# A hybrid DeltaNet and MoBA block: gates and branches computed feature-major, in tiles of 128 features

## The reference, cut to what matters

```python
h = rms_norm(x, norm_pre_w)
proj = jnp.einsum('bsd,df->bsf', h, w_in)          # heads, z paths, 2 x 1024 gate logits
...
gates = sigmoid(gate_logits + b_gate).reshape(bsz, s, 2, d)
pa = jnp.einsum('bsf,fd->bsd', ya, w_branch[0])
pb = jnp.einsum('bsf,fd->bsd', yb, w_branch[1])
merged = gates[:, :, 0] * pa + gates[:, :, 1] * pb
out = jnp.einsum('bsd,de->bse', merged, w_out)
return x + rms_norm(out, norm_post_w)
```

## Time and profile before

| | us |
|---|---|
| median of 3 runs (lowest, highest) | 358.39 (357.66, 358.43) |
| profiled execution, whole | 358.36 |
| profiled execution, span of its instructions | 356.6 |
| PE, DVE, ACT busy | 347.2, 269.1, 219.5 |

### The profile page before, as it was taken

One profiled execution on the slowest core, in us unless ns is written; L12 is line 12 of the kernel. 1 busy time (PEld: TensorE's weight loads), 2 busy tenths in 40 slices (PEclk: granted clock), 3 DMA queues, 4 the chain that ended last, 5 costly groups with the idle time before them and its releaser, 6 DMA issues.

```text
span 356.6 us, 6674 instructions
## 1 busy us (share of the span) xinstructions
PE 347.2 (97%) x2387; PEld 317.9 (89%) x2387; DVE 269.1 (75%) x550; ACT 219.5 (62%) x484; POOL 58.6 (16%) x114
## 2 busy tenths in 40 slices
PE   6999999999999999999999999999999999999993
PEld 5889997888899999999999999999998888888882
DVE  2969877599997868978788797878977657566744
ACT  5778795443447767686867867777776544425421
POOL 1533534500050000300203021030300101000011
PEclk9999999999999999999999999999999999999998
DMA  8766956893599476445744566465534735766333
GB/s 266 175 193 174 342 168 213 232 344 124 141 271 236 122 191 161 123 119 151 203 120 124 135 181 156 119 156 148 169 120 137 247 118 171 245 234 235 123 114 118
DMA packets 76206, 63.48 MB, mean 178 GB/s; under 512 B 4724, under 2 KB 62478, under 8 KB 76174
## 3 DMA queue, kind: packets, MB, share of 16 engines
q1 hardware_dynamic: 73838, 59.37, 57.0%
q0 software_dynamic: 1152, 3.30, 3.2%
q10 hardware_dynamic: 1184, 0.39, 0.5%
HBM read 61.46 MB, written 1.59 MB: 177 GB/s over the span
## 4 chain that ended last, share of the span: by engine, by line
PE 74%; DVE 10%; DMA 6%; ACT 4%; issue 3%; SPq 1%; POOL 1%; DVEq 0%; POOLq 0%; ACTq 0%
PE banks L1387 35%; PE banks L1442 18%; PE banks L1649 6%; DVE w_lo L919 4%; DMA raw<-in_w_in_dram 3%; DMA th_E<-g_rows 2%; PE banks L1405 2%; DVE acc L992 2%; ACT w_hi L670 1%; DVE sub L1056 1%; ACT th_E L711 1%; DMA g_rows<-grow 1%; PE banks L1537 1%; PE banks L1554 1%; PE banks L1543 1%
## 5 line engine op out<-in xcount | busy, mean ns | idle before, releaser
L919 DVE TENSOR_TENSOR w_lo<-raw,w_hi 128x1024 fp32r<-128x1024 f32 x102 | 124.1, 1224 | 47.6 <-ACT w_hi L670 46.9
L670 ACT CAST w_hi<-raw 128x1024 fp32r<-128x1024 f32 x103 | 107.3, 1048 | 30.6 <-PE banks L1442 13.9
L1387 PE MATMUL banks<-h_hi,w_hi 128*128 128x256 f32 x440 | 64.0, 288 | 0.1
L1387 PE MATMUL banks<-h_lo,w_hi 128*128 128x256 f32 x440 | 59.4, 277 | 0.0
L1387 PE MATMUL banks<-h_hi,w_lo 128*128 128x256 f32 x440 | 59.2, 277 | 0.0
L1387 PEld LDWEIGHTS banks<-h_hi,w_hi 128*128 128x128 f32 x440 | 55.2, 189 | 0.7 <-DVE acc L992 0.3
L1387 PEld LDWEIGHTS banks<-h_lo,w_hi 128*128 128x128 f32 x440 | 54.1, 188 | 0.0
L1387 PEld LDWEIGHTS banks<-h_hi,w_lo 128*128 128x128 f32 x440 | 54.1, 188 | 0.0
L992 DVE SCALAR_TENSOR_TENSOR acc<-banks,vec,acc 128x255 f32<-128x255 f32 (+2 forms) x72 | 34.5, 479 | 3.0 <-ACT acc L789 1.3
L616 POOL TENSOR_TENSOR so<-so,rnq 128x2 f32<-128x2 f32 x8 | 2.0, 253 | 162.8 <-ACT junk L856 162.8
L789 ACT ACTIVATE acc<-banks,vec 128x256 f32<-128x256 f32 x16 | 7.6, 475 | 16.9 <-PE banks L1387 16.9
(11 more groups left out here) (257 smaller groups left out, 606.5 us busy)
## 6 DMA issues: line engine op xcount, KB each, us to landing
raw<-in_w_in_dram SPq DMA_DIRECT2D x80, 512.0 KB, 5.1
raw<-in_w_branch_dram SPq DMA_DIRECT2D x16, 512.0 KB, 4.7
raw<-in_w_out_dram SPq DMA_DIRECT2D x8, 512.0 KB, 4.2
xin<-in_x_dram SPq DMA_DIRECT2D x2, 512.0 KB, 3.9
th_E<-g_rows POOLq DMA_DIRECT2D x2, 512.0 KB, 7.3
bias<-bias_rows POOLq DMA_DIRECT2D x1, 1024.0 KB, 7.4
raw<-in_x_dram SPq DMA_DIRECT2D x2, 512.0 KB, 3.7
out_dram<-xin SPq DMA_DIRECT2D x4, 256.0 KB, 2.0
```

What stands on the lines that cost most here:

```text
L670: nc.scalar.copy(w_hi[:, t % SLOTS, :], raw[:, t % SLOTS, :]).then_inc(s_hi, 1)
L919: v.tensor_tensor(w_lo[:, t % SLOTS, cols], raw[:, t % SLOTS, cols], w_hi[:, t % SLOTS, cols].bitcast(F32), ALU.subtract).then_inc(s_lo, 1)
L1387: last = mm(ps, w, r, start=part == 0 and k == 0, stop=part == 2 and k == KT - 1)
```

## The change

Gate and branch tiles become feature-major: each is 128 features, loaded as columns of 512 bytes a row, formed by `third` in banks 0 and 1 in turn, as the heads' tiles are. The gate's bias is then a column: b_gate is loaded as 16 more rows at the start, turned with the other small vectors, scaled by 0.5 on the vector engine, and given to ScalarE's tanh as its bias; the tanh reads the bank directly, 128x256 at a time, 16 times. `gate_front` and its row loads go. Both branches are multiplied tile by tile, the sum is feature-major as it stands, `turn_m` goes, and `m_part` and `m_rest` split 128x256 of it a tile. Waits change with the banks.

```diff
-GATE_ROWS = [(60, 61), (72, 73), (88, 91), (3 * BRANCH0, 3 * BRANCH0 + 1)]
-GATE_TANH = [62, 74, 94, 3 * BRANCH0 + 3]
-M_TURN = 3 * BRANCH0 + 40
...
-        gate_banks = [(bank[0], bank[1]), (bE, bF), (bA, bD), (bC, bank[0])]
-        branch_banks = [(bank[1], bA), (bB, bD), (bE, bF), (bank[0], bank[1])]
-        m_banks = [(bA, bB), (bank[0], bank[1])]
...
+        bgate = sb("bgate", [P, 2 * KT])
...
+        def gate(g):
+            return th_a[:, g, :] if g < KT else th_E[:, g - KT, :]
...
@@ SyncE
             sp.dma_start(rows[R_PRE:R_ON, :], norm_pre_w.rearrange("(t p) -> t p", p=P)).then_inc(s_rows, 16)
-            sp.dma_start(rows[R_ON:ROWS, :], dn_onorm_w.rearrange("(t p) -> t p", p=P)).then_inc(s_rows, 16)
+            sp.dma_start(rows[R_GATE:ROWS, :], b_gate.rearrange("(t p) -> t p", p=P)).then_inc(s_rows, 16)
+            sp.dma_start(rows[R_ON:R_GATE, :], dn_onorm_w.rearrange("(t p) -> t p", p=P)).then_inc(s_rows, 16)
...
-                if n == 12:
-                    sp.wait_ge(s_bd_p, 1)
-                    for group in range(3):
-                        part = b_gate[512 * group:512 * group + 512].rearrange("(a n) -> a n", a=1)
-                        sp.dma_start(early_rows[group], part.to_broadcast([P, 512])).then_inc(s_rows_e, 16)
             for g in range(EARLY):
-                gate_load(GATES_A + g, g // 4, g % 4)
+                load(GATES_A + g, GATES_A + g, w_tile(COL_GATE + P * g))
...
-                half, branch, q = t // 4 % 2, 1 - t // 8, t % 4
-                group_load(BRANCH0 + t, w_branch[branch][256 * q:256 * q + 256, 512 * half:512 * half + 512])
+                k = t % KT
+                load(BRANCH0 + t, BRANCH0 + t, w_branch[1 - t // KT][:, P * k:P * k + P].rearrange("(k p) n -> p k n", p=P))
...
@@ GpSimd
-                if g == HEADS - 1:
-                    pool.wait_ge(s_sc, 2 * HEADS)
-                    pool.dma_start(late_rows, b_gate[1536:2048].rearrange("(a n) -> a n", a=1).to_broadcast([P, 512])
-                                   ).then_inc(s_rows_l, 16)
...
@@ ScalarE
-            def gate_tanh(group):
-                sa.wait_ge(s_gate_b, 2 * group + 2)
-                ac(th[group], th[group], ACT.Tanh, scale=0.5).then_inc(s_gate_th, 1)
-            def m_parts(half, b):
-                sa.wait_ge(s_m_turned, half + 1)
-                k = 4 * half + 2 * b
-                nc.scalar.copy(m_hi[:, k:k + 2, :], m_banks[half][b].rearrange("p (k n) -> p k n", k=2)).then_inc(s_m_hi, 1)
+            def gate_tanh(g):
+                n = GATES_A + g if g < EARLY else GATES_B + g - EARLY
+                sa.wait_ge(s_tile, n + 1)
+                if g == 0:
+                    sa.wait_ge(s_vec, 3)
+                ac(gate(g), bank[n % 2][:, 0:SEQ], ACT.Tanh, bias=bgate[:, g:g + 1], scale=0.5).then_inc(s_gate_th, 1)
+            def m_part(k):
+                sa.wait_ge(s_m_sum, k + 1)
+                nc.scalar.copy(m_hi[:, k:k + 1, :], one(gate(KT + k))).then_inc(s_m_hi, 1)
...
-                for group in range(4):
-                    if S == GATE_TANH[group]:
-                        gate_tanh(group)
-                if S in (M_TURN + 1, M_TURN + 2):
-                    m_parts(0, S - M_TURN - 1)
+                for g in range(2 * KT):
+                    if S == 3 * (GATES_A + g if g < EARLY else GATES_B + g - EARLY) + 3:
+                        gate_tanh(g)
+                for k in range(KT - 1):
+                    if S == 3 * (BRANCH0 + KT + k) + 4:
+                        m_part(k)
                 if part == 1:
                     split_hi(n + LEAD, n + LEAD, (n + LEAD) // SLOTS + 1)
+            m_part(KT - 1)
             for k in range(KT - LEAD):
                 split_hi(OUT0 + k + LEAD, k + LEAD, (OUT0 + k + LEAD) // SLOTS + 1)
...
@@ the vector engine
+            v.tensor_scalar(bgate[:], vec[:, R_GATE:ROWS], 0.5, None, ALU.mult).then_inc(s_vec, 1)
...
+            def second_branch(k):
+                n = BRANCH0 + k
+                ve.wait_ge(s_gate_th, KT + k + 1)
+                ve.wait_ge(s_tile, n + 1)
+                v.scalar_tensor_tensor(out=gate(KT + k), in0=gate(KT + k), scalar=1.0, in1=bank[n % 2][:, 0:SEQ],
+                                       op0=ALU.add, op1=ALU.mult).then_inc(s_m_b, 1)
+            def first_branch(k):
+                n = BRANCH0 + KT + k
+                ve.wait_ge(s_tile, n + 1)
+                v.scalar_tensor_tensor(out=gate(k), in0=gate(k), scalar=1.0, in1=bank[n % 2][:, 0:SEQ],
+                                       op0=ALU.add, op1=ALU.mult).then_inc(s_m_a, 1)
+                ve.wait_ge(s_m_b, k + 1)
+                ve.wait_ge(s_m_a, k + 1)
+                v.tensor_tensor(gate(KT + k), gate(KT + k), gate(k), ALU.add).then_inc(s_m_sum, 1)
+            def m_rest(k):
+                ve.wait_ge(s_m_hi, k + 1)
+                v.tensor_tensor(m_lo[:, k:k + 1, :], one(gate(KT + k)), m_hi[:, k:k + 1, :].bitcast(F32),
+                                ALU.subtract).then_inc(s_m_lo, 1)
...
+                for k in range(KT):
+                    if S == 3 * (BRANCH0 + k) + 3:
+                        second_branch(k)
+                    if S == 3 * (BRANCH0 + KT + k) + 3:
+                        first_branch(k)
+                    if S == 3 * (BRANCH0 + KT + k) + 5:
+                        m_rest(k)
                 if part == 2:
                     split_lo(n + LEAD, n + LEAD)
-            first_branch(1)
+            first_branch(KT - 1)
             for k in range(KT - LEAD):
                 split_lo(OUT0 + k + LEAD, k + LEAD)
-                if k == 2:
-                    m_rest(1)
+                if k == 0:
+                    m_rest(KT - 1)
...
@@ TensorE, bank_free
+                elif n < HEAD0:
+                    if n < GATES_A + 2:
+                        pe.wait_ge(s_tap, 3 * (HEADS - 1 + n - GATES_A))
+                    else:
+                        pe.wait_ge(s_gate_th, n - GATES_A - 1)
...
+                elif n < GATES_B + 2:
+                    pe.wait_ge(s_gz, 2 * HEADS - 1 + n - GATES_B)
+                elif n < BRANCH0 + 2:
+                    pe.wait_ge(s_gate_th, EARLY + n - GATES_B - 1)
+                elif n < BRANCH0 + KT + 2:
+                    pe.wait_ge(s_m_b, n - BRANCH0 - 1)
+                else:
+                    pe.wait_ge(s_m_a, n - BRANCH0 - KT - 1)
...
-                if S == M_TURN:
-                    turn_m(0)
...
+                elif n >= BRANCH0:
+                    branch = 1 - (n - BRANCH0) // KT
+                    if part == 0:
+                        bank_free(n)
+                        if n == BRANCH0:
+                            pe.wait_ge(s_ylo_b, HEADS)
+                        elif n == BRANCH0 + KT:
+                            pe.wait_ge(s_ylo_a, HEADS)
+                    third(n, n, part, y_hi[:, branch], y_lo[:, branch])
...
@@ TensorE, the output
-                if k == 0:
-                    pe.wait_ge(s_m_lo, 2)
+                pe.wait_ge(s_m_lo, k + 1)
...
-                if k == 1:
-                    turn_m(1)
```

More of the change, by code:

```diff
@@ L312, in build @@
         s_m_sum = sem("s_m_sum")
-        s_m_turned = sem("s_m_turned")
         s_m_hi = sem("s_m_hi")
@@ L1202, in branch_done @@
-            def branch_done(group, c):
-                if c == 0:
-                    ve.wait_ge(s_branch_p, group + 1)
-                else:
-                    ve.wait_ge(s_tile, BRANCH0 + 4 * group + 4)
-            def second_branch(half):
-                ve.wait_ge(s_gate_th, (3, 4)[half])
-                for c in range(NC):
-                    branch_done(half, c)
-                    part = th[2 + half][:, c, :]
-                    v.scalar_tensor_tensor(out=part, in0=part, scalar=1.0, in1=branch_banks[half][c], op0=ALU.add,
-                                           op1=ALU.mult).then_inc(s_m_b, 1)
@@ L1219, in first_branch @@
-            def first_branch(half):
-                if half:
-                    ve.wait_ge(s_m_turned, 1)
-                for c in range(NC):
-                    branch_done(2 + half, c)
-                    part = th[half][:, c, :]
-                    v.scalar_tensor_tensor(out=part, in0=part, scalar=1.0, in1=branch_banks[2 + half][c], op0=ALU.add,
-                                           op1=ALU.mult).then_inc(s_m_a, 1)
-                    ve.wait_ge(s_m_a, 2 * half + c + 1)
-                    ve.wait_ge(s_m_b, 2 * half + c + 1)
-                    v.tensor_tensor(m_tok[c], th[2 + half][:, c, :], part, ALU.add).then_inc(s_m_sum, 1)
@@ L1232, in m_rest @@
-            def m_rest(half):
-                for b in range(2):
-                    ve.wait_ge(s_m_hi, 2 * half + b + 1)
-                    k = 4 * half + 2 * b
-                    v.tensor_tensor(m_lo[:, k:k + 2, :], m_banks[half][b].rearrange("p (k n) -> p k n", k=2),
-                                    m_hi[:, k:k + 2, :].bitcast(F32), ALU.subtract).then_inc(s_m_lo, 1)
+            def second_branch(k):
```

(22 more changed lines are left out.)

104 lines of the change are left out of this document (9 added, 95 removed).

## The result

The kernel after took 364.18 us (median of 6 runs, 363.95 to 365.67), the kernel before on the same chip 358.31 (6 runs). The ratio is 1.017, 95% interval 1.0154 to 1.0186: slower by 5.9 us. I had predicted 358.7 in a range of 357.0 to 360.8. The prediction was wrong, and two separate things are in the 5.9 us: the loop that I had forecast, and a slower pace of most of TensorE's products that I had not.

What follows compares the result with a forecast made beforehand. The prediction took TensorE, busy 97% of the span, as the bound. It summed 358.36 - 0.82 - 1.74 - 0.62 + 0.10 + 3.43 = 358.71 and predicted 358.7 us, no measurable change, range 357.0 to 360.8.

Steps and rivals of the forecast that it cites:

- the loop: First branch, tiles 88 to 95: multiply, sum, copy and splits wait in a circle across two engines, 3.44 us a tile; 3.43 lost.
- What bounds the kernel: TensorE, busy 97% of the span, hardly pauses in any stage; in the last stage work removed is gained, waits are paid.
- TensorE's own work: Gate and branch tiles: 96 thirds of a tile at 0.907 us in place of 0.9155, saving 0.8 us.
- narrow products are slower: Rival: all 96 thirds made of 256-column products take 0.03 us more, adding 2.9 us, to 361.6; chance 0.06.
- The turns: Two groups of eight turns in the last stage vanish from TensorE, 0.87 us each, 1.7 us gained together.
- The stall at tiles 30 and 31: Gates: TensorE's wait for the last convolution, behind a bias addition, goes; 0.62 us gained, bounds nothing and 0.6.
- the counter-argument: Gates: tanh before each split delays splits one tile, costing the vector engine some 1 us of 3 gained.
- The start: One more transfer ahead of the first weights, and extra scaling on the vector engine: 0.1 us added, bounds 0 and 0.45.
- DMA: Changed tiles' weights come as 1024 packets of 512 bytes, 2.0 us a tile, under the 2.72 available: cost nothing.

Runs made afterwards that it cites:

- e8: The kernel after with the old addresses of e2 and the loop between ScalarE and the vector engine opened by reordering; 356.27 us.
- e13: e8 with every tensor 128 bytes further on, the weights too; 354.97 us.
- e2: The kernel after with its vectors' table and gate biases allocated last and a hole in their place, so other tensors keep the addresses of before; 360.48 us.
- e1: The kernel before with 128 empty bytes a partition behind its table of vectors, no instruction changed; 362.12 us, ratio 1.0118.
- e10: e8 with x, y and all later tensors 256 bytes further on; 356.28 us.
- e11: e8 with x, y and all later tensors 512 bytes further on; 356.25 us.
- e12: e8 with x, y and all later tensors 768 bytes further on; 355.82 us.
- e14: e8 with only what is allocated ahead of the vectors' table, the weights among it, 128 bytes further on, x and y unmoved; 360.97 us.
- e15: e8 with x, y and later tensors 64 bytes further on, at distance 0 from the weights within 256 bytes; 366.02 us.

## Why the prediction was wrong, step by step

**What bounds the kernel** held. TensorE sets the end in every stage, which is why a few per cent of its pace cost more than any edited instruction.

**TensorE's own work** is the step that failed. I wrote that the 39 clean thirds show 0.907 us and took that pace as a property of the instruction, for the changed tiles and, without a word, for the 64 tiles and the output that the change leaves alone. It depends on where its two operands lie, and on what broke the stream before it. The kernel before had them 192 bytes apart within 256 and the diff's two lines of allocation put them at 64. I read those lines and costed them at nothing. And the sign was in the trace that I read: from 111.00 to 266.24 it has 44 clean thirds and not 39, and two of them, at 117.82 and 131.18, take 0.94. With tile 2 the slow pace stood in three places of the kernel before, where I wrote of one. In e8 and e13, with 192 again, the term is right: the gates' twelve tiles give 0.30 us where I had 36 x 0.0085 = 0.31. In the kernel after the same term and its silent half come to 3.7 us on the other side (after against e2).

The rival "narrow products are slower" pointed at the symptom in the wrong place: it had thirds at 0.94 and a sum of 361.6, but for 96 thirds and because they are narrow, and against it I set a count of 39 thirds that leaves out the two slow ones. In e1 products are slow with no narrow product added. The rule behind it, 2.5 ns beside the columns of each isolated product (the Trainium skill, "TensorE: Matmul & The Clock Gate", section "Back-to-back issue gap"), isn't what acts: in e8 and e13 384 more products take less time than the wide ones did.

**The turns** held: gone from TensorE, and from tile 88 to the end e8 takes 2.0 us less than before, against 1.74 for the turns and 0.2 for narrower branch tiles.

**The stall at tiles 30 and 31** was hit once, by luck. Tiles 28 to 32 should have taken 11.26 us. e13 shows 11.27, the kernel after 11.66 at the slow pace without a wait, e2 and e8 12.19 and 12.15 with a wait of their own a tile earlier, and e10, e11 and e12, which differ from e8 in nothing that the pace shows, 12.49, 12.16 and 11.89. The convolution behind the addition of the bias was not the only thing that made it late; I had given up the counter-argument (splits that begin a tile later) too easily.

**The start** was inside its bounds and is nothing that can be read: tile 1 starts 0.29 later in the kernel after and 0.01 to 0.24 earlier in e2, e8 and e13, which have the same loads.

**The loop** was the right mechanism and too small. Its period is 3.51 and not 3.44, nearly all of it in multiply to sum (0.53, not 0.45). Opening it at the fast pace gives 4.0 us from tile 88 to the end (e2 against e8), where I had 3.43; seven periods at 0.07 more are 0.5 of that. At the slow pace it cost 3.2, since TensorE's own 2.83 a tile hides more of it. The first wait came at tile 94 there; at the fast pace of e2 it comes at tile 93, 3.05 behind tile 92 in place of 2.72, as I had drawn it.

**DMA** held at nothing: in the branches ScalarE waits once for a load (2.36 us at 307.46; 2.1 us before), and TensorE doesn't wait there.

With the operands at their old distance the sum would have missed too, by less: e2 took 360.48 against 358.71. The slow tiles 24 to 28 are 0.5 of it, the stall 0.9, the loop 0.6; the start gave 0.4 back; 0.2 isn't accounted for.

**Would the idea have paid?** Yes, twice repaired: with the loop opened and the operands at 192 it takes 354.97 to 356.28 us, 0.5% to 0.9% less than before, with the turns and the bias rows gone as the change wanted.

## What to carry to other kernels

When a stage that the change doesn't touch takes another time, look first at what the change moved in memory, and compare the pace of the same instruction in the same stage of both traces. An allocation is an edit: keep new tensors behind the operands of the hot products, or test the kernel before with nothing but the new addresses, which is one line. When two in-order engines each do two jobs a step, draw the chain through both queues; if it closes on itself, its period is the sum of the starts' distances, and swapping two instructions that need not be in that order opens it.

## What the runs showed of the hardware that I had not expected

The pace of a product of 256 columns depends on the addresses of its two operands against each other, modulo 256 bytes. In the branches eight take 0.907 us at a distance of 192, 0.942 at 64, 0.947 to 0.949 at 128, 160 and 224, and 0.960 at 0, that is 113 to 120 ns each, at a mean granted clock of 0.995 to 0.999. At 192 and at 64 both 0.907 and 0.942 occur (129 and 6 clean thirds in e8, 21 and 117 in e14), and the pace changes almost only where something breaks the stream.

The Trainium skill says of TensorE, on the page "SBUF — State Buffer", section "SBUF: two separate sides", that it never waits on anyone, and in the section "A bandwidth-pool intuition that's wrong (but worth ruling out)" that the loading of weights has a read port of its own. The runs disagree with what a reader would take from that: from e13 to e14 no instruction changes, x, y and all that is allocated with them move by 128 bytes and the weights stay, and the pace changes by 4%. That the two reads get in each other's way is the obvious guess; no run here shows it, since the records of the narrow products' weight loads have a mean of 188 or 189 ns in e13, e14 and the kernel after alike (190 to 192 in e15).
